# Second layer: value, key and query projections of the middle stage as split tiles, and a written-out order for the tiles between them

## The reference, cut to what matters

```
h = rms_norm_2(x, attn_norm) * (1.0 + scale_a) + shift_a
(nq, nkc, nvc, nks, nvs, nkw, nvw, ngate, cq, ckv, kr, bgate) = jnp.split(h @ w_in, IN_OFFSETS, axis=-1)
kc = rms_norm_2(compress(rope(heads(nkc, G), pos), cmp_k_pe, cmp_k_w1, cmp_k_w2), nsa_kc_norm)
vc = compress(heads(nvc, G), cmp_v_pe, cmp_v_w1, cmp_v_w2)
g_nsa = jax.nn.sigmoid(heads(ngate, NSA_HEADS))
q_b = (rms_norm_2(cq, mla_cq_norm) @ w_uq).reshape(B, S, MLA_HEADS, MLA_QK_DIM)
kv_b = (rms_norm_2(ckv, mla_ckv_norm) @ w_ukv).reshape(B, S, MLA_HEADS, MLA_NOPE_DIM + MLA_V_DIM)
```

## Time and profile before

| what | value |
|---|---|
| median of 3 runs | 1662.79 us (1661.13 to 1663.99) |
| the profiled execution | 1662.53 us |
| its span in the profile | 1660.7 us |
| TensorE busy in the span | 1620.8 us, 98% |
| VectorE, ScalarE, GpSimd busy | 76%, 50%, 10% |
| HBM read | 309.71 MB, 190 GB/s over the span |

### The profile page before, as it was taken

One profiled execution on the slowest core, in us unless ns is written; L12 is line 12 of the kernel. 1 busy time (PEld: TensorE's weight loads), 2 busy tenths in 40 slices (PEclk: granted clock), 3 DMA queues, 4 the chain that ended last, 5 costly groups with the idle time before them and its releaser, 6 DMA issues.

```text
span 1660.7 us, 32559 instructions
## 1 busy us (share of the span) xinstructions
PE 1620.8 (98%) x11538; PEld 1430.8 (86%) x11538; DVE 1255.8 (76%) x2664; ACT 823.8 (50%) x1500; POOL 162.5 (10%) x134
## 2 busy tenths in 40 slices
PE   6999999999999999999999999999999999999998
PEld 4887988899988878888888888888889777999998
DVE  6885538759989988788888888888858256588887
ACT  3544111365469845555555555555744255544443
POOL 0020000017700000000000000000057014100000
PEclk9999999999999999999999999999999999999999
DMA  9742135855642288777777777777545651345553
GB/s 353 288 147 89 41 119 205 321 193 176 223 133 64 97 262 269 232 235 237 236 236 238 240 235 240 235 238 237 181 134 161 220 172 39 98 143 178 186 181 127
DMA packets 102625, 316.98 MB, mean 191 GB/s; under 512 B 11392, under 2 KB 21376, under 8 KB 102144
## 3 DMA queue, kind: packets, MB, share of 16 engines
q1 hardware_dynamic: 101664, 311.27, 56.3%
q10 hardware_dynamic: 864, 4.39, 0.7%
HBM read 309.71 MB, written 5.90 MB: 190 GB/s over the span
## 4 chain that ended last, share of the span: by engine, by line
PE 54%; DVE 15%; issue 14%; ACT 12%; DMA 2%; DVEq 1%; SPq 1%; POOL 0%; ACTq 0%
PE bank L501 9%; PE bank L502 9%; PE bank L503 9%; ACT whi L490 6%; DVE xn L2201 3%; PE bank L1301 3%; DVE Wlo L2184 2%; DVE arena L2190 2%; DVE wlo L495 2%; ACT arena L2031 2%; PE bank L2068 2%; PE bank L2070 2%; PE bank L2072 2%; PE bank L476 2%; PE bank L1587 2%
## 5 line engine op out<-in xcount | busy, mean ns | idle before, releaser
L490 ACT CAST whi<-wring 128x1024 fp32r<-128x1024 f32 x386 | 403.4, 1046 | 156.9 <-PE bank L503 84.7
L495 DVE TENSOR_TENSOR wlo<-wring,whi 128x1024 fp32r<-128x1024 f32 x341 | 415.3, 1223 | 52.2 <-ACT whi L490 42.8
L501 PE MATMUL bank<-xboth,whi 128*128 128x256 f32 x1032 | 296.9, 288 | 3.9 <-DVE wlo L495 2.2
L502 PE MATMUL bank<-xboth,whi 128*128 128x256 f32 x1032 | 291.9, 283 | 0.0
L503 PE MATMUL bank<-xboth,wlo 128*128 128x256 f32 x1032 | 291.9, 283 | 0.0
L501 PEld LDWEIGHTS bank<-xboth,whi 128*128 128x128 f32 x1032 | 197.8, 192 | 8.7 <-issue 3.8
L502 PEld LDWEIGHTS bank<-xboth,whi 128*128 128x128 f32 x1032 | 197.9, 192 | 0.7 <-issue 0.5
L503 PEld LDWEIGHTS bank<-xboth,wlo 128*128 128x128 f32 x1032 | 197.8, 192 | 0.0
L495 POOL TENSOR_TENSOR wlo<-wring,whi 128x1024 fp32r<-128x1024 f32 x45 | 114.9, 2560 | 811.7 <-ACT whi L490 811.6
L514 PE MATMUL bank<-xboth,whi 128*128 128x512 f32 x704 | 188.7, 390 | 0.0
L2068 PE MATMUL bank<-whi,Whi 128*128 128x512 f32 x512 | 159.7, 393 | 2.9 <-DVE Wlo L2184 2.9
(11 more groups left out here) (397 smaller groups left out, 2889.8 us busy)
## 6 DMA issues: line engine op xcount, KB each, us to landing
wring<-in_w SPq DMA_DIRECT2D x463, 512.0 KB, 3.5
arena<-in_ada SPq DMA_DIRECT2D x48, 512.0 KB, 7.4
xn<-in_ada SPq DMA_DIRECT2D x96, 256.0 KB, 2.7
h_spill<-arena SPq DMA_DIRECT2D x37, 128.0 KB, 1.7
arena<-h_spill SPq DMA_DIRECT2D x37, 128.0 KB, 3.9
wring<-in_w SPq DMA_DIRECT2D x6, 384.0 KB, 4.8
wring<-in_w SPq DMA_DIRECT2D x8, 256.0 KB, 3.3
arena<-in_const ACTq DMA_DIRECT2D x1, 1215.0 KB, 5.5
```

The lines of the kernel that those rows point to most:

```text
L490: act.copy(whi[:, n % HSLOTS, :], wring[:, n % SLOTS, :]).then_inc(hi_ready, 1)
L495: eng.tensor_tensor(wlo[:, n % SLOTS, :], wring[:, n % SLOTS, :], whi[:, n % HSLOTS, :].bitcast(F32), ALU.subtract).then_inc(lo_ready, 1)
L501: pe.matmul(out, h, xh, start=start, stop=False, **kw)
L502: pe.matmul(out, h, xl, start=False, stop=False, **kw)
```

## The change

The four value tiles leave `w_in2` and become `tok 0` to `tok 3` of `MIX`, repacked: each now holds four of the eight row blocks of a pair's 256 columns, and two tiles fill one PSUM bank (`tokens`, 24 fp32r matmuls of 256 columns for each tile). They, `uk`, `uq` and `uv` become split tiles (the 18 of `LIFT`): ScalarE casts each (`act_lift_hi`, placed in its list behind the copy of the tile three before), GpSimd makes all lower halves (`lift_lo`), and TensorE makes three products for each block. The activations of the ranks are split too: ScalarE casts five blocks into `xhi` once `tok 3` is done (`act_ranks_upper`), VectorE subtracts (`dve_ranks_rest`), and `uk 0` waits for that. The gate tile `gt` stays plain and moves behind `cmp_k 6`. The 16 compression tiles are dealt out by a written list, `sums` and `give` move as in the diff, `give(1)` is cut in three pairs and one, and no `cmp_v` tile is left behind `give(2)`. The number of tiles (67 from the first of `w_in2` to the last of `MIX`) and of bytes is the same.

```diff
-          ("w_in2", 43 - LATE), ("mix", 30), ("late", LATE),
+          ("w_in2", 38 - LATE), ("mix", 35), ("late", LATE),
...
-BESIDE = [("cmp_k", t) for t in range(8)] + [("cmp_v", t) for t in range(8)]
-MIX = [tile for pair in zip([(name, t) for name in ("uk", "uq", "uv") for t in range(COUNT[name])], BESIDE)
-       for tile in pair] + BESIDE[14:]
+COUNT.update(tok=4, gt=1, uk=4, uq=6, uv=4)
+MIX = ["tok 0", "cmp_k 0", "tok 1", "cmp_k 1", "cmp_k 2", "tok 2", "cmp_k 3", "cmp_k 4", "tok 3", "cmp_k 5", "cmp_k 6",
+       "gt 0", "cmp_k 7", "uk 0", "uk 1", "cmp_v 0", "uk 2", "uk 3", "cmp_v 1", "uq 0", "cmp_v 2", "uq 1", "cmp_v 3",
+       "uq 2", "uq 3", "cmp_v 4", "uq 4", "cmp_v 5", "uq 5", "uv 0", "cmp_v 6", "uv 1", "cmp_v 7", "uv 2", "uv 3"]
...
+LIFT = [tile for tile in MIX if tile[0] == "tok" or tile[0] in WIDTH]
...
-            pe.wait_ge(xn_ready, 3 * KT)
-            for k in range(SPLIT2, COUNT["w_in2"]):
-                n, r = first + k, ring0 + k
-                pe.wait_ge(landed[n % SLOTS], count_at(n))
-                pe.wait_ge(ring_free, r - BANKS + 1)
-                matmul8_tokens(pe, bank[r % BANKS], n % SLOTS).then_inc(tile_done, 1)
...
+            def leave_tokens(p):
+                tile_wait(act, "tok", 2 * p + 1)
+                act.copy((vs2, vw2)[p], ring_bank("tok", p)[:, :].rearrange("p (b f) -> p b f", b=TT)).then_inc(ring_free, 1)
...
+            act_lift_hi(act, 2)
+            leave(SPLIT2 - 1)
+            act_lift_hi(act, 3)
+            leave_tokens(0)
+            leave_tokens(1)
+            act_ranks_upper(act)
+            act_lift_hi(act, 4)
+            act_lift_hi(act, 5)
+            tile_wait(act, "gt", 0)
+            act.activation(gt2[:, :, :], ring_bank("gt", 0)[:, 0:S].rearrange("p (b f) -> p b f", b=TT)[:, :, 0:24],
+                           ACT.Sigmoid).then_inc(ring_free, 1)
+            act_lift_hi(act, 6)
...
+        def lift_slot(j):
+            return (FIRST["w_in2"] + SPLIT2 + j) % HSLOTS
+
+        def act_lift_hi(act, j):
+
+            if j < len(LIFT):
+                n, w = MIX_AT[LIFT[j]], WIDTH.get(LIFT[j][0], D)
+                act.wait_ge(landed[slot_of(n)], count_at(n))
+                act.wait_ge(tile_done, (MIX_AT[LIFT[j - HSLOTS]] if j >= HSLOTS else FIRST["w_in2"] + SPLIT2 + j - HSLOTS) + 1)
+                act.copy(whi[:, lift_slot(j), 0:w], wring[:, slot_of(n), 0:w]).then_inc(hi_ready, 1)
+
+        def lift_lo(eng):
+
+            for j, tile in enumerate(LIFT):
+                n, w = MIX_AT[tile], WIDTH.get(tile[0], D)
+                eng.wait_ge(hi_ready, nth_split[n])
+                eng.tensor_tensor(wlo[:, slot_of(n), 0:w], wring[:, slot_of(n), 0:w], whi[:, lift_slot(j), 0:w].bitcast(F32),
+                                  ALU.subtract).then_inc(lo_ready, 1)
+
+        def act_ranks_upper(act):
+
+            act.wait_ge(c_n, 1)
+            tile_wait(act, "tok", 3)
+            act.copy(xhi[:, 0:5, :], F2[:, 16:21, :]).then_inc(x_hi, 1)
+
+        def dve_ranks_rest(dve):
+
+            dve.wait_ge(x_hi, XHI[3])
+            dve.tensor_tensor(xlo[:, 0:5, :], F2[:, 16:21, :], xhi[:, 0:5, :].bitcast(F32), ALU.subtract).then_inc(x_lo, 1)
...
+            dve_ranks_rest(dve)
...
+            def tokens(t, n, bk):
+                for i in range(4):
+                    k = 4 * (t % 2) + i
+                    h, l = whi[:, lift_slot(t), i * S:(i + 1) * S], wlo[:, slot_of(n), i * S:(i + 1) * S]
+                    for b in range(TT):
+                        out, rows = bk[:, b * S:(b + 1) * S], slice(b * 128, (b + 1) * 128)
+                        pe.matmul(out, xhi[:, k, rows], h, start=(k == 0 and b == 0), stop=False, skip_group_check=True)
+                        pe.matmul(out, xlo[:, k, rows], h, start=False, stop=False, skip_group_check=True)
+                        mm = pe.matmul(out, xhi[:, k, rows], l, start=False, stop=(k == KT - 1), skip_group_check=True)
+                return mm
+
+            def lifted(j, n, k, x, xl, out, first, last):
+                h, l = whi[:, lift_slot(j), k * 128:k * 128 + 128], wlo[:, slot_of(n), k * 128:k * 128 + 128]
+                pe.matmul(out, h, x, start=first, stop=False)
+                pe.matmul(out, h, xl, start=False, stop=False)
+                return pe.matmul(out, l, x, start=False, stop=last)
+
+            def uq(j, n, bk):
                 for o in range(2):
                     for k in range(3):
-                        mm = pe.matmul(bk[:, o * S:(o + 1) * S], blocks(slot, 3 * o + k), F2[:, 16 + k, :],
...
+                        mm = lifted(j, n, 3 * o + k, xhi[:, k, :], xlo[:, k, :], bk[:, o * S:(o + 1) * S], k == 0, k == 2)
...
+                if name == "tok":
+                    pe.wait_ge(lo_ready, nth_split[n])
+                    pe.wait_ge(ring_free, RING0["tok"] + t // 2 - BANKS + 1)
+                    tokens(t, n, ring_bank("tok", t // 2)).then_inc(tile_done, 1)
+                elif name == "gt":
+                    pe.wait_ge(xn_ready, 3 * KT)
+                    pe.wait_ge(landed[slot_of(n)], count_at(n))
+                    pe.wait_ge(ring_free, r - BANKS + 1)
+                    token(slot_of(n), bank[r % BANKS]).then_inc(tile_done, 1)
+                else:
+                    pe.wait_ge(lo_ready, nth_split[n])
+                    pe.wait_ge(ring_free, r - BANKS + 1)
+                    dict(uk=uk, uq=uq, uv=uv)[name](LIFT.index((name, t)), n, bank[r % BANKS]).then_inc(tile_done, 1)
...
+                if (name, t) == ("uk", 0):
+                    pe.wait_ge(x_lo, XLO[3])
                 if name in COUNT:
                     up(name, t)
                 else:
                     pe_compress(pe, name == "cmp_v", name, t)
                 if (name, t) == ("uk", 1):
                     turned_key()
-                elif (name, t) == ("cmp_k", 5):
+                elif (name, t) == ("uq", 1):
                     sums(1, 8)
-                elif (name, t) == ("cmp_k", 7):
-                    give(1)
+                elif (name, t) == ("uq", 3):
+                    give(1, 0, 1, 2)
                 elif (name, t) == ("uq", 4):
                     pe.wait_ge(l_k, 1)
+                    give(1, 3)
                 elif (name, t) == ("uv", 0):
                     pe_fold(pe, 0)
                 elif (name, t) == ("uv", 1):
                     pe_compressed(pe, 0)
                     sums(2, None)
-                elif (name, t) == ("cmp_v", 4):
-                    give(2)
+                elif (name, t) == ("uv", 2):
+                    give(2, 0, 1, 2, 3)
...
+                act_lift_hi(act, 4 + t + 3)
...
+                act_lift_hi(act, 8 + t + 3)
...
+                act_lift_hi(act, 14 + t + 3)
...
+            lift_lo(pool)```

ScalarE's list in `act_mla`, from the copies of `uq` 2 and 3 on, before (L2772 and L2777 copy a tile of `uq` and of `uv`, L2524 and L2532 belong to the compression, L2783 is the root):

```order
L2772 COPY arena<-bank 128x512 [waits tile_done] x2
L2524 COPY arena<-bank 128x256 [waits tile_done]
L2772 COPY arena<-bank 128x512 [waits tile_done] x2
L2777 COPY arena<-bank 128x2x256 [waits tile_done]
L569 ACT_TABLE_LOAD
L569 ACTIVATE part<-cols 128x1 [waits tables]
L2532 ACTIVATE arena<-bank 128x60 [waits cm_t]
```

More of the change, by code:

```diff
@@ L55 @@
 WIDTH = {"uq": 768, "uk": 512, "uv": 512}
-COUNT.update(uk=4, uq=6, uv=4)
-BESIDE = [("cmp_k", t) for t in range(8)] + [("cmp_v", t) for t in range(8)]
-MIX = [tile for pair in zip([(name, t) for name in ("uk", "uq", "uv") for t in range(COUNT[name])], BESIDE)
-       for tile in pair] + BESIDE[14:]
+COUNT.update(tok=4, gt=1, uk=4, uq=6, uv=4)
+MIX = ["tok 0", "cmp_k 0", "tok 1", "cmp_k 1", "cmp_k 2", "tok 2", "cmp_k 3", "cmp_k 4", "tok 3", "cmp_k 5", "cmp_k 6",
+       "gt 0", "cmp_k 7", "uk 0", "uk 1", "cmp_v 0", "uk 2", "uk 3", "cmp_v 1", "uq 0", "cmp_v 2", "uq 1", "cmp_v 3",
+       "uq 2", "uq 3", "cmp_v 4", "uq 4", "cmp_v 5", "uq 5", "uv 0", "cmp_v 6", "uv 1", "cmp_v 7", "uv 2", "uv 3"]
+MIX = [(tile.split()[0], int(tile.split()[1])) for tile in MIX]
 MIX_AT = {tile: FIRST["mix"] + i for i, tile in enumerate(MIX)}
-RINGED = ["w_in", "gates1", "proj", "w_out", "wq", "w_in2", "uk", "uq", "uv", "late", "w_o"]
+RINGED = ["w_in", "gates1", "proj", "w_out", "wq", "w_in2", "tok", "gt", "uk", "uq", "uv", "late", "w_o"]
 RING0 = {}
@@ L66 @@
     RING0[_name] = _n
-    _n += COUNT[_name]
+    _n += COUNT[_name] // (2 if _name == "tok" else 1)
 SLOTS = 6
@@ L480, in build_layer_pair @@
         x_hi, x_lo = sem("x_hi"), sem("x_lo")
-        split_tiles = [FIRST[name] + k for name in SPLIT for k in range(SPLIT2 if name == "w_in2" else COUNT[name])
+        split_tiles = [MIX_AT[LIFT[k]] if name == "lift" else FIRST[name] + k
+                       for name in SPLIT for k in range(len(LIFT) if name == "lift" else COUNT[name])
                        if k >= SKIP.get(name, 0) or (name == "peer" and k < EARLY_SPLIT and k != EARLY_PLAIN)]
@@ L2302, in leave @@
```

(36 more changed lines are left out.)

30 lines of the change are left out of this document (16 added, 14 removed).

## The result

| | median | lowest to highest | ratio to the kernel before, 95% interval |
|---|---|---|---|
| kernel before, same runs | 1662.62 us (20 runs) | 1660.99 to 1663.99 | |
| changed kernel | 1665.81 us (20 runs) | 1662.59 to 1670.79 | 1.0022 [1.0016, 1.0028] |

The changed kernel is 3.2 us slower, at the very edge of what the prediction called "no change". Not only the median moved: the runs of before spread over 3.0 us, those of after over 8.2. That spread turns out to be the better clue. The profiled execution took 1667.12 us with a span of 1665.3.

The account below looks back on a forecast made before the run. TensorE was taken to bound the stage; what counts is when `give(2)` begins. Products -9.9, switches +2.5 and moved compression tiles +1.7 make -5.7 us, waits and restarts +5.7: about 1662.8 us, no change, range 1659.0 to 1666.8.

Parts of the forecast that it names:

- no change: Whole kernel: a time between 1659.5 and 1666.1 us, about 0.2% either way; chance 0.66.
- Products: TensorE ahead of `give(2)`: split matmuls of 256 columns at 0.12 us shorten value, `uk`, `uq` and `uv` tiles, 9.9 us less.
- Waits: TensorE up to `give(2)`: six waits in one chain add up to 5.4 us, plus 0.3 for restarts.
- `tok 3`: Eighth tile after `tok 0`, requested late: landed, cast and subtracted at T + 13.8, TensorE there at T + 12.0; 1.9 us.
- the silu: At `pe_compressed`: ScalarE's cast of `uv 3` stands ahead of the silu's table load, so TensorE waits 1.4 us.
- The sum to `give(2)`: `give(2)` within 2.5 us of T + 60.7, T being the start of `tok 0`'s first product.
- the switches and restarts: TensorE ahead of `give(2)`: 25 edges between split and plain products cost 2.5 us, restarts behind the waits 0.3.
- The chain behind `give(2)`: VectorE's four scalings from `give(2)` to the attention's first maxima keep their 8.0 us.
- The rate of DMA: Sign in the new trace: DMA moves above 270 GB/s over the stage.
- Rival 2: Ring of six tile slots becomes the bound; at 250 GB/s later tiles come late, +3.5 us, 1666.3; chance 0.10.
- rival 3: Port lock with GpSimd delays VectorE's list, so key scaling and `uq` tiles come later: +3 us, 1665.8; chance 0.10.
- Under the chain now lies `uv 3` alone: Behind `give(2)`: three compression tiles move ahead of it, 1.7 us back; VectorE's chain amply covers `uv 3`.

Follow-up runs that it names:

- experiment 2: The changed kernel with ScalarE's cast of `uv 3` moved from ahead of the silu's table load to behind the silu: 1664.16 us, ratio 1.0016.
- experiment 7: The changed kernel with VectorE's square of the first six query blocks put behind the third pair of key scalings: 1666.77 us, ratio 1.0035.
- experiments 1 to 4: Changed kernel with filler ahead of the scores, cast behind silu, or `tok 2`, `tok 3` earlier; kernel before with last compression tiles ahead of `give(2)`: 1.0015, 1.0016, 1.0023, 1.0014.
- experiment 1: The changed kernel with eight unused TensorE products of 128 columns in the idle gap ahead of the attention's third scores product: 1664.48 us, ratio 1.0015.
- experiment 8's first: The changed kernel with 24 filler products ahead of `tok 3` (5.6 us, meant as 1.3) and eight ahead of the scores: 1665.93 us, ratio 1.0030.
- Experiment 9: The changed kernel with the cast of `uv 3` behind the silu, eight fillers ahead of the scores and seven ahead of `tok 3`: 1661.97 us, ratio 1.0003.
- the control of 5: The kernel before with only the eight filler products of 128 columns added ahead of the scores: 1662.68 us, ratio 1.0004.

## Why the prediction was right or wrong

**The range held, the forecast was 3 us low.** 1665.81 lies within 1659.0 to 1666.8. The interval of the ratio, +0.16 to +0.28%, covers the line of 0.2% between "no change" and "slower".

**Products: right.** `uk` 1.61 us (1.45 to 1.65 said), `uq` 2.34 (2.2 to 2.4), `tok` 2.97 to 3.07 with edges (2.9 to 3.1).

**Waits: right in place and nearly in size.** Said and measured: `tok 3` 1.9 and 1.7, `uq` 0.5 and 0.6, `give(1)` 0.6 and 0.3, its last pair 0.8 and 0.5, the silu 1.4 and 1.4, `give(2)` 0.2 and 0.3; in all 5.4 and 4.9. (Two of the forecast terms don't follow from their own parts: 5.6 less 4.1 makes 1.5 for the silu, and 2.25 against 2.21 makes nothing for `give(2)`.) Shown as causes: the silu's, by experiment 2 (it goes when the cast moves). That of `tok 3` begins with a landing, as the prediction's chain said. ScalarE's cast, idle before it for its weights:

```profile
1292.36 1.05 ACT L2582 CAST whi<-wring 128x1024 fp32r<-128x1024 f32 x1 [5.21 <-DMA wring<-in_w]
```

T + 9.9, where 10.2 was said.

**The sum to `give(2)`: 0.6 us off.** T + 61.3, where 60.7 was said. The waits were 0.5 less than said, so the switches and restarts cost more than their 2.8, about 3.9; this I only infer from the difference. **The chain behind `give(2)`: right**, 8.0 us.

**The rate of DMA: wrong.** "Above 270 GB/s over the stage" was 259 and 227 in the two stretches above, and 241 from T to `give(2)`. The line contradicts the prediction's own sum: 241 GB/s over 61.3 us are 14.8 MB, and the same bytes in the 60.7 us that it forecast make 244. So the low rate says little about how fast the transfers could have gone. Rival 2 (the ring as the bound) foresaw +2 us at `uq 1` and more at `uq 3` to `uq 5`; there only 0.6 us of waiting was seen, ahead of `uq 1`. Of rival 3 the collision itself was seen (3195 ns against 1759), but with it `give(2)` still came within 0.6 us of the forecast, and moving the square in experiment 7 won nothing. Its total of 1665.8 is the measured one by luck: the +3 us that it put ahead of `give(2)` are not there.

**The step that failed** is this sentence: "Under the chain now lies `uv 3` alone, so there is more than enough cover for it." I had asked whether TensorE's tiles would delay the chain, and they do not. I had not asked what TensorE does when they are done. It stands idle for 2.27 us instead of 1.29, and in the profiled execution its clock falls to 1.2 GHz behind that: 3.2 us more from the scores to the end. The same holds for the wait for `tok 3`, which I had priced at its length alone. None of the rivals had this, so that the measured time lies in the range owes nothing to its mechanism. All six waits were priced as time lost once; by the runs an idle stretch of 1.5 to 2.9 us costs its length, and in some executions another 1.4 to 1.7, or 3.2 us, behind it.

**How the +3.2 us divides.** The runs bound it and do not settle it. By the mean clocks, 0.9973 over the changed kernel's 20 runs and 0.9989 over the kernel before's 35 of experiments 1 to 4, the clock's part is 0.0016 of 1663 us, 2.7 us; these clocks are rounded to a thousandth and come from different runs, so this is an estimate. By the runs at a full clock it is less: experiment 1's runs at 0.999 and experiment 8's first, after its overrun, both keep 1.7 us over the kernel before, which leaves 1.5 for the clock. Experiment 9 against 2 lies between, with 1.9 to 2.2. Of the 1.7 us the profiles show 1.0: the scores come 0.6 us later, and the way from them to the end is 0.4 longer. The other 0.7 may be a cost of the fillers, which both kernels carry (the control of 5 lies 0.7 above the kernel before, within its interval), for the changed kernel's own two runs at 0.999 have a mean of 1662.9, only 0.3 above it. It isn't settled.

**What stays open.** Why the clock falls in one execution and not in the next of the same kernel: with 2.3 us of idle time it fell in the profile of the changed kernel and not in that of experiment 2. And the changed kernel was never run with both idle stretches filled at the right size and nothing else changed. No version was found that beats the kernel before: the best is level with it. In the changed kernel, what TensorE saves ahead of `give(2)`, 4.3 us (busy for 56.4 where it was busy for all of 60.7), meets 4.9 us of waits.

## What to carry to other kernels

When a change shortens the bounding engine's work, look not only for what waits longer on the path, but for every stretch in which TensorE now has nothing to do, those under another engine's chain too: cover that is too short costs as well as cover that is too long. A spread of run times that grows from 3 to 8 us is a result in itself; sort the runs by their mean granted clock before you look for a cause in one profile. And size a filler from a row of the same products (0.235 us each here), not from their columns.
